# Hand-written schedule of a two-block transformer kernel: work moved between ScalarE, VectorE and GpSimd in the first attention, and reordered in the layer norm chain and the second attention

## The reference, cut to what matters

```python
h = depthwise_conv(h) + dw_b                    # first block
h = silu(layernorm(h, ln_g, ln_b)) @ pw2_w + pw2_b
...
p = softmax(q @ k.T * scale - slope * dist)     # 16 heads, a selected and a window branch
o = gate_slc * (p_slc @ v_slc) + gate_win * (p_win @ v_win) + gate_cmp * (p_cmp @ v_cmp)
...
mh = mlstm(q, k, v, i, f)                       # second block
mh = mh * rsqrt(mean(mh * mh) + EPS) * ml_norm * sigmoid(o)
p = softmax(q @ k.T * scale + c_i - c_j)        # forgetting attention, 8 heads
x = x + concat(mh, p @ v) @ w_out
```

## Time and profile before

| | before |
|---|---|
| median of 3 runs | 1100.76 us (1100.59 to 1102.19) |
| the profiled execution's own time | 1104.01 us |
| its span | 1102.3 us |
| instructions | 17103 |
| TensorE busy | 1045.1 us (95% of the span) |
| VectorE busy | 670.9 us (61%) |
| ScalarE busy | 500.7 us (45%) |
| GpSimd busy | 65.6 us (6%) |
| share of TensorE in the chain that ended last | 82%, VectorE 10%, ScalarE 3% |
| HBM | 157 GB/s over the span |

### The profile page before, as it was taken

How to read it: one execution, slowest core, us unless ns; L and a number is a source line. 1 busy time by engine, 2 the same in 40 slices (tenths; PEclk the granted TensorE clock), 3 DMA queues, 4 the chain that set the end, 5 groups by cost and what they waited for, 6 DMA issues and landing times.

```text
span 1102.3 us, 17103 instructions
## 1 busy us (share of the span) xinstructions
PE 1045.1 (95%) x7233; PEld 929.5 (84%) x7233; DVE 670.9 (61%) x1021; ACT 500.7 (45%) x713; POOL 65.6 (6%) x109
## 2 busy tenths in 40 slices
PE   5997999999999889999999999999879999999997
PEld 5984799999989846899999989988658989999996
DVE  3997456555567598655555568757654446455554
ACT  5424444343453466645444354544543445444432
POOL 2000193000000000000000001000000000000000
PEclk9998999999999989999999999999979999999999
DMA  8883556666636401657666646545134425656540
GB/s 225 218 216 94 153 154 202 197 175 191 191 85 198 146 1 40 210 171 211 191 187 177 198 128 212 172 141 191 42 112 152 154 73 176 210 170 209 159 150 39
DMA packets 188999, 174.28 MB, mean 158 GB/s; under 512 B 12822, under 2 KB 164502, under 8 KB 188922
## 3 DMA queue, kind: packets, MB, share of 16 engines
q1 hardware_dynamic: 187216, 169.67, 50.1%
q10 hardware_dynamic: 1322, 2.62, 0.7%
q0 software_dynamic: 384, 0.90, 0.2%
HBM read 171.24 MB, written 1.93 MB: 157 GB/s over the span
## 4 chain that ended last, share of the span: by engine, by line
PE 82%; DVE 10%; ACT 3%; issue 2%; DMA 2%; ACTq 0%; SPq 0%; POOLq 0%; POOL 0%; DVEq 0%
PE bank L1792 25%; PE bank L1793 24%; PE bank L1794 24%; DVE split_lo L1073 2%; PE bank L1981 2%; ACT split_hi L662 2%; DVE xn_lo L1090 1%; DMA pt<-in_cmp_pos_v 1%; PE bank L1829 1%; DVE soft L1390 1%; DMA raw<-in_a_pw_w 1%; DVE soft L1403 1%; ACT xn_hi L700 1%; PE bank L2144 1%; PE bank L2345 0%
## 5 line engine op out<-in xcount | busy, mean ns | idle before, releaser
L1073 DVE TENSOR_TENSOR split_lo<-raw,split_hi 128x2048 fp32r<-128x2048 f32 (+1 forms) x157 | 356.6, 2276 | 190.4 <-ACT split_hi L662 190.1
L1792 PE MATMUL bank<-xn_hi,split_hi 128*128 128x256 f32 x1456 | 415.4, 285 | 5.7 <-DVE xn_lo L1090 5.1
L1793 PE MATMUL bank<-xn_lo,split_hi 128*128 128x256 f32 x1456 | 411.8, 283 | 0.0
L1794 PE MATMUL bank<-xn_hi,split_lo 128*128 128x256 f32 x1456 | 411.8, 283 | 0.0
L662 ACT ACTIVATE split_hi<-raw 128x2048 fp32r<-128x2048 f32 (+1 forms) x157 | 296.5, 1892 | 127.8 <-PE bank L1794 120.4
L1792 PEld LDWEIGHTS bank<-xn_hi,split_hi 128*128 128x128 f32 x1456 | 278.0, 191 | 11.9 <-issue 4.4
L1793 PEld LDWEIGHTS bank<-xn_lo,split_hi 128*128 128x128 f32 x1456 | 278.2, 191 | 1.5
L1794 PEld LDWEIGHTS bank<-xn_hi,split_lo 128*128 128x128 f32 x1456 | 278.1, 191 | 0.0
L1792 PE MATMUL bank<-split_hi,ffa_hi 128*128 128x512 f32 x320 | 125.3, 392 | 1.8 <-DVE ffa_lo L1073 1.8
L1793 PE MATMUL bank<-split_lo,ffa_hi 128*128 128x512 f32 x320 | 124.9, 390 | 0.0
L1794 PE MATMUL bank<-split_hi,ffa_lo 128*128 128x512 f32 x320 | 124.5, 389 | 0.0
(11 more groups left out here) (306 smaller groups left out, 928.1 us busy)
## 6 DMA issues: line engine op xcount, KB each, us to landing
raw<-in_ffn_w_in SPq DMA_DIRECT2D x88, 512.0 KB, 5.2
raw<-in_w_ff SPq DMA_DIRECT2D x32, 1024.0 KB, 5.4
raw<-in_ffn_w_out SPq DMA_DIRECT2D x22, 1024.0 KB, 4.9
raw<-in_w_in SPq DMA_DIRECT2D x14, 1024.0 KB, 5.3
raw<-in_a_pw_w SPq DMA_DIRECT2D x16, 512.0 KB, 8.2
raw<-in_w_xkv SPq DMA_DIRECT2D x8, 1024.0 KB, 5.7
raw<-in_a_pw_w SPq DMA_DIRECT2D x4, 1024.0 KB, 8.7
raw<-in_b_w_in SPq DMA_DIRECT2D x4, 1024.0 KB, 6.1
```

What stands on the lines that cost most here:

```text
L1073: return nc.vector.tensor_tensor(dst, src, hi.bitcast(F32), ALU.subtract)
L1792: mm(dst, left[0], right[0], start=start, stop=False)
L1793: mm(dst, left[0], right[1], start=False, stop=False)
L1794: return mm(dst, left[1], right[0], start=False, stop=stop)
```

## The change

Three places, and a renaming (`pt_dve` becomes `pt_first`, `pt_act` becomes `pt_second`).

First attention: piece 0 of each head's weights (128x128) is weighed by GpSimd, in place, with its own semaphore `pool_weighed`, for which `nsa_turn` waits too; VectorE weighs pieces 1 to 3. The copy out of bank 4 is ScalarE's for even heads (in front of its copy out of bank 5) and stays VectorE's for odd heads.

```diff
-        DVE_PIECES = [0, 1, 2, 3]
+        POOL_PIECE, DVE_PIECES = 0, [1, 2, 3]
...
-            for k in (NSA, FFN1, MEM, MID, IN2):
+            root(NSA)
+            for i in range(HEADS):
+                pool.wait_ge(inverse_ready, i + 1)
+                part, n = scores_of(i)[:, NSA_PIECES[POOL_PIECE]], POOL_PIECE
+                nc.gpsimd.tensor_scalar(part, part, rcol[:, i % 2, n:n + 1], gate_of(n, i), ALU.mult,
+                                        ALU.mult).then_inc(pool_weighed, 1)
+            for k in (FFN1, MEM, MID, IN2):
                 root(k)
...
-                nc.scalar.activation(dst[:, 384:768], bank[5][:, 0:384], ACT.Copy).then_inc(pt_act, 1)
+                if i % 2 == 0:
+                    nc.scalar.activation(dst[:, 0:384], bank[4][:, 0:384], ACT.Copy).then_inc(pt_first, 1)
+                nc.scalar.activation(dst[:, 384:768], bank[5][:, 0:384], ACT.Copy).then_inc(pt_second, 1)
...
-                nsa_evac(2 * p)
                 if p == 1:
                     cmp_weigh(1)
...
             def nsa_turn(i):
                 te.wait_ge(weighed, i + 1)
+                te.wait_ge(pool_weighed, i + 1)
```

```diff
+            through(chunk_of["pw2"][2])
             conv_evac(3)
             conv_evac(4)
-            through(chunk_of["pw2"][2])
             square_about_pivot(0)
             square_about_pivot(1)
+            square_about_pivot(2)
             conv_evac(5)
-            square_about_pivot(2)
             square_about_pivot(3)
...
             centre(0)
-            centre(1)
             ve.wait_ge(std_ready, 1)
             link(nc.vector.reciprocal(ln_rstd, ln_rstd))
...
             normalise(0)
+            centre(1)
             normalise(1)
...
-            for ft in CONV_DVE:
+            for ft in CONV_DVE + CONV_PE[5:]:
                 channel_sum(ft)
             te.wait_ge(pads_zero, 2)
             te.wait_ge(squares_summed, 1)
             for ft in (0, 1, 6):
                 square_sum(ft, 3)
-            channel_sum(CONV_PE[5])
             square_sum(7, 4).then_inc(stat_done, 1)
```

```diff
                 if i % 2 == 0 and i:
                     out_hi(HEADS + i, ffa[0][:, i // 2 - 1, :], bank[1 + 2 * ((i // 2 - 1) % 2)][:, 0:S])
+                if i % 2 and i > 1:
                     through(chunk_of["xkv_v"][2] + i // 2)
                 if i % 4 >= 2:
                     memory_evac(4 + 2 * (i // 4) + i % 4 - 2)
...
                 if i % 2 and i > 1:
                     fx_out(i // 2 - 1)
-                    through(chunk_of["xkv_v"][2] + i // 2)
+                if i in (0, 4, 6, 7):
+                    through(chunk_of["xkv_v"][2] + (0, 4, 6, 7).index(i))
                 if i == 1:
-                    through(chunk_of["xkv_v"][2])
...
+                    recurrent_square()
+                if i == 2:
+                    recurrent_norm()
+                if i == 3:
+                    recurrent_gate()
...
             fx_scores(0)
-            memory_values(0)
             for j in range(FXH // 2):
                 if 2 * j + 2 < FXH:
                     fx_scores(j + 1)
                 fx_turn(2 * j)
-                memory_values(2 * j + 1)
+                memory_values(2 * j)
                 if j:
                     fx_pv(j - 1)
                 fx_turn(2 * j + 1)
-                if 2 * j + 2 < FXH:
-                    memory_values(2 * j + 2)
+                memory_values(2 * j + 1)
             fx_pv(FXH // 2 - 1)
```

More of the change, by code:

```diff
@@ L305, in build_kernel @@
         weighed = sem("weighed")
+        pool_weighed = sem("pool_weighed")
         p_turned = sem("p_turned")
-        pt_dve = sem("pt_dve")
-        pt_act = sem("pt_act")
+        pt_first = sem("pt_first")
+        pt_second = sem("pt_second")
         pv_done = sem("pv_done")
@@ L974, in fx_evac @@
                 nc.scalar.activation(fx_weights(i), bank[6 + i % 2][:, 0:3 * P],
-                                     ACT.Copy).then_inc(pt_act, 1)
+                                     ACT.Copy).then_inc(pt_second, 1)
             fx_exp(0)
@@ L1025, in x_evac @@
                     sc.wait_ge(pv_done, n - 1)
-                nc.scalar.activation(pt[:, i % 2, 0:512], bank[6 + i % 2][:, :], ACT.Copy).then_inc(pt_act, 1)
+                nc.scalar.activation(pt[:, i % 2, 0:512], bank[6 + i % 2][:, :], ACT.Copy).then_inc(pt_second, 1)
             def x_out_hi(i):
@@ L1412, in nsa_evac @@
                     nc.vector.tensor_copy(cmp_t[:, CMP_TURN.index(i), 0:P], bank[4][:, 384:512])
-                nc.vector.tensor_copy(dst[:, 0:384], bank[4][:, 0:384]).then_inc(pt_dve, 1)
+                nc.vector.tensor_copy(dst[:, 0:384], bank[4][:, 0:384]).then_inc(pt_first, 1)
             def nsa_out(ft):
@@ L1674, in _, with recurrent_square, recurrent_norm, recurrent_gate @@
                                     ).then_inc(ml_copied, 1)
+            def recurrent_square():
+                ve.wait_ge(act_link, 4)
+                nc.vector.tensor_reduce(den[:, 3, :], mlsq, AX.X, ALU.add).then_inc(ml_sq, 1)
+            def recurrent_norm():
+                ve.wait_ge(ml_rstd, 1)
+                link(nc.vector.tensor_tensor(num[:, :, 0:MLD], num[:, :, 0:MLD],
+                                             den[:, 5, :].unsqueeze(2).broadcast_to([P, 8, MLD]), ALU.mult))
+            def recurrent_gate():
+                for t in range(TT):
+                    nc.vector.tensor_tensor(numv[:, t, :, 0:MLD], numv[:, t, :, 0:MLD],
+                                            mlo[:, t, :].rearrange("p (h c) -> p h c", h=MLH),
+                                            ALU.mult).then_inc(ml_out, 1)
             for i in range(FXH):
@@ L1681, in _ @@
                     fx_out(i // 2 - 1)
-                    through(chunk_of["xkv_v"][2] + i // 2)
+                if i in (0, 4, 6, 7):
+                    through(chunk_of["xkv_v"][2] + (0, 4, 6, 7).index(i))
                 if i == 1:
-                    through(chunk_of["xkv_v"][2])
-                    ve.wait_ge(act_link, 4)
-                    nc.vector.tensor_reduce(den[:, 3, :], mlsq, AX.X, ALU.add).then_inc(ml_sq, 1)
-                if i == 4:
-                    ve.wait_ge(ml_rstd, 1)
-                    link(nc.vector.tensor_tensor(num[:, :, 0:MLD], num[:, :, 0:MLD],
-                                                 den[:, 5, :].unsqueeze(2).broadcast_to([P, 8, MLD]), ALU.mult))
-                    for t in range(TT):
-                        nc.vector.tensor_tensor(numv[:, t, :, 0:MLD], numv[:, t, :, 0:MLD],
-                                                mlo[:, t, :].rearrange("p (h c) -> p h c", h=MLH),
-                                                ALU.mult).then_inc(ml_out, 1)
+                    recurrent_square()
[3 more added lines that the diff above has]
+                    recurrent_gate()
             fx_out(FXH // 2 - 1)
@@ L2132, in nsa_turn @@
                 te.wait_ge(weighed, i + 1)
+                te.wait_ge(pool_weighed, i + 1)
                 if i:
-                    te.wait_ge(pt_dve, i)
-                    te.wait_ge(pt_act, i)
+                    te.wait_ge(pt_first, i)
+                    te.wait_ge(pt_second, i)
                 s = scores_of(i)
@@ L2147, in nsa_pv @@
             def nsa_pv(p):
-                te.wait_ge(pt_dve, 2 * p + 2)
-                te.wait_ge(pt_act, 2 * p + 2)
+                te.wait_ge(pt_first, 2 * p + 2)
+                te.wait_ge(pt_second, 2 * p + 2)
                 if p >= 2:
@@ L2292, in fx_turn @@
                 if i >= 2:
-                    te.wait_ge(pt_act, n - 1)
+                    te.wait_ge(pt_second, n - 1)
                 else:
@@ L2303, in fx_pv @@
             def fx_pv(j):
-                te.wait_ge(pt_act, HEADS + 2 * j + 2)
+                te.wait_ge(pt_second, HEADS + 2 * j + 2)
                 if j >= 2:
@@ L2370, in x_pv @@
             def x_pv(i):
-                te.wait_ge(pt_act, HEADS + FXH + i + 1)
+                te.wait_ge(pt_second, HEADS + FXH + i + 1)
                 for half in range(2):
```

## The result

The changed kernel took 1090.0 us (median of 4 runs, 1089.69 to 1092.31), the kernel before beside it 1101.47 (4 runs, 1100.59 to 1105.82): a ratio of 0.9894, 95% interval [0.9868, 0.992]. The forecast was 1090.2. The profiled execution of after is 1092.31 us long (span 1090.6), so 2.3 us above its median; between the two profiled executions lie 11.7 us, of which 10.6 were forecast. The total hides terms that were off, and they are what the experiments are about. By a fall I mean a stretch in which TensorE's granted clock goes from its upper level to its lower one (2.4 to 1.2 GHz, 1.00 to 0.50 in the windows).

A forecast was written before the change was run, and what follows sets the result against it. TensorE, busy for 95% of the span, was taken as the bound. Gains of 9.5, 1.0 and 0.1 make 10.6 us off 1104.01, so 1093.4; less 3.25 for the median, 1090.2 us, range 1085.8 to 1095.2.

The forecast's parts named there:

- Second attention: Second attention: the product out2 starts 9.0 us earlier; with the clock's gains and losses behind it, 9.5 us saved.
- the tail: End of the second attention, fx_pv(3), transposes, high and low parts: 4.1 us instead of 4.94, one clock fall charged 1.5.
- lower bound of 6.5: Second attention: gain if the early waits bring a clock fall too and the tail takes 4.94 us.
- Layer norm chain: Layer norm chain: variance 1.45 us earlier; between 0.6 and 1.45, a gain of 1.0 us was taken.
- the 0.8 to be given back: End of the layer norm chain: TensorE perhaps still at half clock after its earlier restart, giving back 0.8 us.
- First attention: First attention: period 6.31 against 6.22, four periods losing 0.1 each, 0.5 brought ahead of them; gain 0.1 us.
- L: First attention: lag by which GpSimd's piece ends behind VectorE's three, taken as 0.4 us, added to a 5.91 us period.
- A: Rival: second attention gives only half, 5 us, through a fall by an early wait or late turn(4); 1094.7 us, chance 0.15.
- B: Rival: all at the good end, GpSimd beside VectorE, no fall in the tail; 14.2 us gained, 1086.5 us, chance 0.12.
- C: Rival: in the first attention GpSimd lags by 1 us or more, 2.6 lost there; 1092.9 us, chance 0.08.
- D: Rival: in the first attention GpSimd's piece is blocked repeatedly and every nsa_turn waits, 14 us lost; 1104.3 us, chance 0.03.
- E: Rival: second attention's moved fillers only move the waits, and L eats the rest; 1100.5 us, chance 0.02.

The follow-up runs named there:

- p_even: Kernel before with only the even heads' evacuation in the first attention moved from VectorE to ScalarE: 1100.28 us, ratio 0.9976.
- v_two_inputs: Changed kernel with VectorE's three weighings written as scalar_tensor_tensor, with two tensor inputs instead of one: 1091.11 us, ratio 0.9904.
- v_tail: Changed kernel with the eight transposes of the recurrent output in front of memory_values(7), their copies ahead of the last splits: 1087.76 us, ratio 0.9873.
- v_both: v_tail with block 0 of memory_values back behind fx_scores(0) and the transposes in front of turn(7): 1087.73 us, ratio 0.9874.
- v_front: Changed kernel with TensorE's memory_values blocks back in their old places, ScalarE's and VectorE's order staying changed: 1092.15 us, ratio 0.9915.
- p_nsa: Kernel before with both edits of the first attention alone: 1100.33 us, ratio 0.9975.
- v_swap: Changed kernel with VectorE's reciprocal and weighing of head 2p+2 in front of head 2p+1's evacuation and the output's low part: 1090.76 us, ratio 0.9892.
- p_ln: Kernel before with the edits of the layer norm chain alone: 1103.19 us, ratio 1.0002.
- v_wide: Changed kernel with GpSimd weighing piece 2, of 256 columns, instead of piece 0, of 128: 1091.18 us, ratio 0.99.
- p_pool: Kernel before with only GpSimd's weighing of piece 0, VectorE keeping the even heads' evacuation: 1098.37 us, ratio 0.9969.
- v_best: v_both with VectorE's order of v_swap, and memory_evac(7) in front of ScalarE's split in the second attention: 1084.58 us, ratio 0.9836.
- p_fx: Kernel before with the edits of the second attention alone: 1098.29 us, ratio 0.9945.

## Why the prediction came out right, and where it did not

**Second attention, 9.5 forecast, 8.9 measured between the two profiles.** The layout held almost block by block: out2 at 42.15 us after `fx_scores(0)`, laid out at 41.5; no wait in the loop; the tail 3.99 us (809.39 to 813.38), forecast 4.1, with its fall (the 30 matmuls behind it took 8.51 us against 6.95 without one, so 1.56, charged 1.5). The term that was off is the front: the bounds had "if the early waits bring one too", and they did, in every profile that has this front (0.57 in after between 776 and 780). That is about 1.2 us by turn(0) to turn(1), 4.38 us instead of 3.18. A wait of 0.5 for weigh(1), which I had charged, did not come. (The lower bound of 6.5 does not follow from its terms: 9.5 less 1.5 for that fall and 0.8 for the tail is 7.2.) And the 8.9 owe something to the profile of before, in which the old order met the lower clock more than elsewhere: over the five kernels of each order the stage and the 30 matmuls behind it took 57.5 and 50.4 us on average (54.6 to 59.7, and 50.2 to 50.7), so 7.1 is the better estimate of what the reordering is worth.

**Layer norm chain, 1.0 forecast.** 1.54 at the restart, forecast 1.45: right, though the row was misread, for TensorE restarts at 102.06 in before, and the 105.11 that the prediction took for it is the seventh matmul behind that. Of the 0.8 to be given back the pair of profiles shows 0.6, but over all profiles the part behind the restart is only 0.1 us longer with the edit and scatters by more than 1; so that term is not borne out, and 1.5 is the better estimate of the whole.

**First attention, 0.1 forecast, 4.1 measured.** This is the step that failed, in two terms. L was taken at 0.4 from the row in which GpSimd stood for 3.22 us beside VectorE's split; it is 0, and the period is the 5.91 of "5.91, plus the lag L". A period of 5.9 was one of the prediction's own signs of being wrong. (That it is exact is partly chance: the path was 6.10 and not 6.16, as p_even shows, and the piece gave 0.20 and not 0.25, since three pieces took 1.05 us and four 1.25.) Four periods at 0.31 make 1.2 us, where 0.4 had been charged. The row was the nearest, but it was a longer instruction beside a much longer one with two tensor inputs; the weighings have one, and even v_two_inputs stretched GpSimd by 0.32 only. Which of length and form made the 3.22 was not tried. The rule of the Trainium skill that I weighed (Perfetto Trace Analysis, Optimizing Scalar/DVE Operations) says that the two engines share a port, which a two-port VectorE operation locks, so that moving work between them might not help. Here it helped, the period fell by 0.31 us. That the two engines hold each other up is seen in both forms, 0.84 instead of 0.52 us for GpSimd in one and 0.06 us on VectorE in the other, but no run shows whether the weighings are two-port operations. The second term was larger: "Ahead of them, where turn(1), (3) and (4) wait for VectorE alone, the evacuation and piece saved bring 0.5". The three stretches that end on these turns went from 12.79 to 11.15 us, so 1.6: the piece is saved on each of them and an evacuation on the first two. The prediction's own prices, three pieces at 0.25 and two evacuations at 0.47, make 1.7; the 0.5 was mis-sized. Another 0.7 us is the clock between turn(1) and turn(2), on which the prediction had nothing and which v_tail, v_both and v_front did not repeat. The last 0.6 us lie behind turn(12), where the prediction had nothing either. Over the five kernels with just these edits here (after, p_nsa, v_tail, v_both, v_front) the stage took 66.1 us on average, over the three without any 69.9: 3.7 is the better estimate.

**The sum** came out because 4.0 us too little here met 0.6 too much in the second attention and 1.7 and 0.5 us lost on stretches without an edit. That it lies within 0.2 us of the forecast is luck: the errors cancelled. The start-up loss is the clock: 0.66 between 25 and 30 us in after, 1.00 in before. Without those two the pair would have been 13.9 us apart, near the good end of the range (1104.01 less 13.9 less the 3.25 that I took off for the median is 1086.9; the low end was 1085.8).

**Rivals.** A (half of the second attention, 5 us): its condition, a fall by an early wait, came, but it cost 1.2 us; turn(4) was not late, and the stage gave 8.9 between the two profiles and 7.1 on average. Only against the quickest profile of the old order (p_nsa) would it be 4, so 5 is unlikely and not excluded. B was nearer in the first attention (GpSimd beside VectorE), but it had no fall in the tail, and that fall came. C and D, a lagging GpSimd, are excluded: its piece ends 0.46 us ahead of VectorE's. E is answered by v_front: the blocks' places are worth 0.9 us beside the moved splits and norm, so E was nearly right about the fillers and wrong about the change, which moved more than them.

**Open.** The parts timed alone (ratios less 1: -0.55, +0.02 and -0.25%) add up to some 8.6 us with about 4 of uncertainty, the whole is 11.5. That is no contradiction within these intervals. The averages of the stretches, 7.1, 1.5 and 3.7 us, add up to 12.3, inside the interval of the whole (8.8 to 14.5). The clock at the start differed between the profiled executions by up to 3 us without an edit there; whether that goes with the kernel or with the execution was not tried.

## What to carry to other kernels

Find what stands in the queue in front of the instruction that a wait ends on: here three of the four waits of 1.5 to 2.7 us ended on something small behind a 2 us split, and moving the splits, with the norm, was worth far more than moving fillers on the waiting engine. Where two engines bound a loop within 0.1 us, work out both lines and take from the one that is a chain; then ask whether an instruction has to be in that chain at all (v_swap took 0.4 us off a period with no instruction less). When executions scatter by more than a part is worth, cut the traces at fixed instructions and compare stretches: those without an edit show what a stretch can tell.

## What was not expected of the hardware

- The same wait brings the lower clock in one execution and not in another. A wait of 1.3 to 2.0 us for a load near 23.6 us was followed, between 25 and 30 us, by a granted clock of 1.00 (before, p_even, v_two_inputs, v_tail, v_both), 0.66 to 0.74 (after, p_ln, v_wide, p_nsa, p_pool, v_best) and 0.50 (p_fx, v_swap), which cost 0, about 1.5 and 3.1 us (`conv(5)` ended at 90.7 to 90.9, 91.9 to 92.7, and 93.9 us); v_front, which did not wait there, kept 1.00. The old second attention lay between 47.7 and 50.7 us in the same way, at a granted clock of 0.96 to 0.88. Its length did not decide: 1.80 us (p_even) brought nothing, 1.29 (v_best) did.
- GpSimd's weighing cost 0.52 us for 128 columns and 0.62 for 256. The second 128 columns cost only 0.10, yet an instruction of 8 columns took 0.20 us and one of 384 took 1.17, so these four do not lie on one line. Beside it, VectorE's one-input weighings kept their length but for the second of a head, which was 0.06 us longer beside GpSimd's 128 columns and 0.17 beside its 256. Whether the weighings slow GpSimd isn't known: no run has it alone.
